# Attention projections on one core: queries stored per head, the first steps and the query pass in another order, weights' low parts on GpSimd

## The chip, the cores and the metric

The kernel runs as one program on one core of a Trainium2 chip. The metric is device time in microseconds (us), smaller is better. "Before" is the kernel as it stood, "after" the changed one. All times in this part come from the kernel before.

## The reference

Sequence 2048 plus 16 learned meta tokens in front (T = 2064), width 1024. Layer one is latent attention with a gate, layer two a gated short convolution; each ends in a layer norm with a residual.

```python
proj = h @ w_in                                    # 1024 -> 384 + 256 + 32 + 1024
c_q, c_kv, k_rope, z = split(proj)
q = (rms_norm(c_q, g_q) @ w_uq)                    # 16 heads x (64 + 32)
q = [q_nope, rope(q_rope)]
c_kv = rms_norm(c_kv, g_kv)
k_nope, v = c_kv @ w_uk, c_kv @ w_uv               # 16 heads x 64 each
k = [k_nope, rope(k_rope)]                         # one rope key for all heads
p = softmax(q k^T / sqrt(96), block-causal over chunks of 64)
out = (p v * silu(z)) @ w_o
h = layer_norm(alpha * h + out)
# then: in-projection to 4 x 1024, gates, a causal width-3 convolution, out-projection, layer norm
```

## The kernel before

Float32 products are made as three products of parts: a high part (`hi`, the value rounded to the engine's narrower format) and a low part (`lo = value - hi`); `split_matmul` (L41) issues hi x hi, hi x lo and lo x hi, all on TensorE. So every operand, inputs and weights, must be split before it is used: ScalarE (ACT) writes the high part as a copy, VectorE (DVE) subtracts for the low part.

Five stages follow one another: `stage_p` (projections), `stage_b` (attention), `stage_c` (output projection), `stage_d` and `stage_e` (the convolution layer). The change is in `stage_p` and in how `stage_b` loads queries.

**stage_p.** The 2064 tokens are eight chunks of 258 columns (`CA`, `NCA`). `STEPS_P` orders the work as p0, p1, o0, p2, o1, p3, o2, ...: step "p g" projects chunk g into the latents (three banks of 24 matmuls of 258 columns: `project`), step "o g" makes the outputs of pass g from its latents (`make`). g 0 to 7 is the key pass (two latent tiles and the rope key; eight key tiles and four or more value tiles out), g 8 to 15 the query pass (three latent tiles; eight query tiles "q" and four rope tiles "r" out), then eight "z" steps make the gates. Outputs go through a ring of four PSUM banks: output r waits until output r-4 has been taken out of its bank, by ACT or by DVE (`TAKER`), into one of eight stage slots, which the SP queue stores to DRAM. In the query pass the order is q q r q q r ...; ACT takes the q, DVE the r (four multiplications with the cos and sin tables `rot`).

Between p and o lies a chain over several engines: ACT copies the banks (`copies`), DVE squares (`squares`), TensorE sums over partitions (`mean_squares`), DVE adds epsilon (`mean_taken`), ACT takes the root (`root`), DVE inverts (`inverse`), does a Newton step of four operations (`newton`) and scales (`normalise`), ACT makes the high part and DVE the low part (`latent`). Each engine runs its instructions in the order in which they are written, so this order, with the waits in it, is written out by hand. For the rope key, DVE multiplies by cos and sin (`rotate_key`), ACT moves the sin half, DVE subtracts, and SP stores it (L299).

The cos and sin tables are made on the chip: a chain of DVE operations from the positions (L628 to L639), then four Sin activations on ACT (L405). In the kernel before they come ahead of the first step, and `copies(0)`, which frees the first banks, comes behind them on ACT.

The weights come in 30 pieces (`PIECES`), loaded by SP into four quarter buffers; the load of a piece waits until the piece before it in that buffer has its low part (`PIECE_FREE`, semaphore `w_split`). GpSimd (POOL) does nothing in this stage but two memsets.

**stage_b.** Per head, SP loads keys, then queries (four transfers: 64 plain rows, 32 cos rows, 16 and 16 sin rows) and values; GpSimd splits them for the next head while the current one runs. TensorE, ACT and DVE run in a written-out order. Each unit's output is added by DVE (L1165) into one of two halves of a buffer that SP stores (L910); the next but one waits for that store.

Of the kernel before, what the change touches and what calls it, by code (L numbers as in the profile page):

```python
# [6 lines left out]
F32 = mybir.dt.float32  # L7
F32R = mybir.dt.float32r
I32 = mybir.dt.int32
ALU = mybir.AluOpType  # L10
# [3 lines left out]
P = 128  # L14
# [140 lines left out]
FIRST_KEYS = 96  # L155
KEYS_IN, KEYS_SPLIT, QUERIES_IN, QUERIES_SPLIT = 2 * NCA + 1, 2 * NCA + 3, 2 * NCA + 4, 2 * NCA + 6


def load_queries(sp, raw, h, queries, semaphore):

    qn_d, qc_d, qs_d = queries
    at = 32 * (h % 4)
    sp.dma_start(raw[0:64, :], qn_d[h // 2, 64 * (h % 2):64 * (h % 2) + 64, :]).then_inc(semaphore, 16)
    sp.dma_start(raw[64:96, :], qc_d[h // 4, at:at + 32, :]).then_inc(semaphore, 16)
    sp.dma_start(raw[96:112, :], qs_d[h // 4, at + 16:at + 32, :]).then_inc(semaphore, 16)
    sp.dma_start(raw[112:P, :], qs_d[h // 4, at:at + 16, :]).then_inc(semaphore, 16)
# [9 lines left out]
def stage_p(nc, own, dram):  # L176

    x_a, w_x, w_uk, w_uv, w_uq, pos, rope_c, gains, ident_d, k_d, kr_d, v_d, queries, z_d = dram
# [3 lines left out]
    with ExitStack() as ctx:  # L182
# [70 lines left out]
        def _(sp):  # L253
# [14 lines left out]
            def store(r):  # L268
                kind, g, what, m, half, _ = OUTS[r]
                sp.wait_ge(taken[TAKER[r]], TAKEN[r])  # L270
                if what == "v":
                    t0, rows = value_tiles(g)[m]
                    to = v_d[t0:t0 + rows, half * HALF:half * HALF + HALF]
                else:
                    to = {"k": k_d, "q": queries[0], "r": queries[1], "z": z_d}[what][m, :, chunk_cols(g)]
                sp.dma_start(to, stage_of(r, rows_of(r))).then_inc(stored[SLOT[r]], 16)
                if what == "r":
                    sp.dma_start(queries[2][m, :, chunk_cols(g)], sines_of(r)).then_inc(stored[SLOT[r] + 1], 16)
# [11 lines left out]
            for i in range(3, 7):  # L290
                load_piece(i)
            next_piece = 7
            for kind, g in STEPS_P:
                if kind == "p":
                    if g == 1:
                        load_x(2)
                    if g < NCA:
                        sp.wait_ge(k_sum, g + 1)
                        sp.dma_start(kr_d[:, chunk_cols(g)], krs[0:32, :]).then_inc(kr_out, 16)  # L299
# [12 lines left out]
                if kind == "z" and g == KEYS_IN:  # L312
# [6 lines left out]
                    sp.dma_start(rot[96:P, :], kr_d).then_inc(first_in, 16)  # L319
# [3 lines left out]
                if kind == "z" and g == QUERIES_IN:  # L323
                    sp.wait_ge(first_split, 2)
                    load_queries(sp, rot, 0, queries, first_in)
# [8 lines left out]
        def _(pool):  # L334
            nc.gpsimd.memset(means[:, 0, :], 1.0 / KVL).then_inc(consts_set, 1)
            nc.gpsimd.memset(means[:, 1, :], 1.0 / QL).then_inc(consts_set, 1)

        @block.scalar
        def _(act):
# [17 lines left out]
            def copies(g):  # L357
                for j in range(tiles_of(g)):
# [3 lines left out]
                    nc.scalar.activation(craw[:, j, :], banks[:, j, 0:CA], ACT.Copy).then_inc(c_taken, 1)  # L362
                if g < NCA:
                    act.wait_ge(k_turned, g + 1)
# [28 lines left out]
            def first_queries():  # L393
                act.wait_ge(first_in, FIRST_KEYS + 64)
# [7 lines left out]
            act.wait_ge(angle, 1)  # L402
            for half in range(2):
                for part in range(2):
                    nc.scalar.activation(rot[64 * part:64 * part + 32, half * HALF_T:half * HALF_T + HALF_T],  # L405
                                         ang[64 * half + 32 * part:64 * half + 32 * part + 32, :], ACT.Sin).then_inc(sined, 1)
            for kind, g in STEPS_P:
                if kind == "p":
                    if g:
                        split_x(g + 1)  # L410
                    if g == 1:
                        root(0)
                        latent(0)
                    if g != 1:
                        split_weights(PIECES_AT.get((kind, g), ()))
                    copies(g)
                    if g == 1:
                        split_weights(PIECES_AT[kind, g])
# [30 lines left out]
        def _(pe):  # L449
            def bank_free(g, j):  # L450
# [3 lines left out]
                if g <= NCA and j == KKV:  # L454
                    pe.wait_ge(k_turned, g)
# [79 lines left out]
        def _(dve):  # L535
# [11 lines left out]
            def split_weights(pieces):  # L547
                for name, n in pieces:
                    i = PIECE[name, n]
                    dve.wait_ge(w_hi_done, i + 1)  # L550
                    nc.vector.tensor_tensor(piece_to(i, 1), piece_raw(i), piece_to(i, 0).bitcast(F32), ALU.subtract).then_inc(w_split, 1)
# [7 lines left out]

            def rotate_key(g):  # L560
                dve.wait_ge(proj, 3 * g + 3)
                if g == 0:
                    dve.wait_ge(sined, 4)
                for part in (0, 64):
                    last = nc.vector.tensor_tensor(kt[part:part + 32, :], banks[part:part + 32, 2, 0:CA], rot[part:part + 32, chunk_cols(g)], ALU.mult)
# [58 lines left out]
            split_weights([("x", 0)])  # L624
            split_half_x0(1)
            split_weights([("x", 1)])
# [4 lines left out]
            split_weights([("x", 2)])  # L631
            for part in (TURN1, TURN2, TURN3):
                then(nc.vector.scalar_tensor_tensor(ang, turns, -part, ang, ALU.mult, ALU.add))
            split_x(1)
            then(nc.vector.tensor_scalar(ang, ang, rc[:, 2:3], None, ALU.add))
# [4 lines left out]
            for kind, g in STEPS_P:  # L640
                extra = list(PIECES_AT.get((kind, g), ()))
                if kind == "p":
                    if g:
                        split_x(g + 1)
                    if g == 1:
# [3 lines left out]
                        normalise(0)  # L649
                        latent(0)  # L650
                    if g != 1:
                        split_weights(extra)
                    squares(g)
# [1127 lines left out]
```

## Time and profile before

| what | us |
|---|---|
| median of 3 runs | 2818.47 (2814.31 to 2821.31) |
| the profiled execution's own time | 2829.5 |
| span of its instructions | 2827.7 |
| TensorE's matmuls busy in the span | 2660.8 (94%) |
| VectorE, ScalarE, GpSimd busy | 1597.0 (56%), 1219.4 (43%), 752.2 (27%) |
| stage_p in it | 0 to about 618 |
| stage_b in it | about 618 to 1670 |

The profile is of one execution. PE is TensorE's matmuls, PEld its weight loads, SPq the transfer queue of SyncE. A row of the timeline gives start, duration, engine, line, operation, what it writes and reads, and in brackets how long the engine had been idle and what released it. "x2" merges neighbours.

### The profile page before, as it was taken

The numbers are of one execution on the slowest core, as the hardware profiler recorded it, in microseconds if no ns is written. First come the engines' busy times: TensorE is split into PE (matmuls) and PEld (weight loads), VectorE is DVE, ScalarE is ACT, GpSimd is POOL, SyncE is SP. The second block draws the span as 40 slices with busy tenths as digits, with TensorE's granted clock in tenths as the row PEclk, the third lists the DMA queues.
The fourth block names the chain that finished last, engine by engine and source line by source line (L and its number), as shares of the span: only waits on it lengthen the run. The fifth ranks groups of instructions, "written<-read, shape, count | busy, mean of one in ns | idle before, by whom it ended". The sixth has DMA issues, their size and how long they took to land. (4 is left out here: it accounts for less than half of the span.)

```text
span 2827.7 us, 45472 instructions
## 1 busy us (share of the span) xinstructions
PE 2660.8 (94%) x16756; PEld 2434.5 (86%) x16756; DVE 1597.0 (56%) x3262; ACT 1219.4 (43%) x3055; POOL 752.2 (27%) x332
## 2 busy tenths in 40 slices
PE   5998899999999999999999979969999999999898
PEld 5898899999888989898989858859988899889686
DVE  5556571129888878898988848854112111121465
ACT  4333222238887878887878841112111001110211
POOL 0000000013344544433444204441211111211244
PEclk8999999999999999999999989989999999999999
DMA  4545344312243334333333335643111011110543
GB/s 139 187 152 170 123 140 137 106 45 47 49 92 82 87 77 90 80 73 69 78 70 70 62 106 166 190 157 105 37 45 37 22 37 37 37 31 17 175 154 113
DMA packets 235457, 260.88 MB, mean 92 GB/s; under 512 B 86992, under 2 KB 188240, under 8 KB 228880
## 3 DMA queue, kind: packets, MB, share of 16 engines
q1 hardware_dynamic: 217600, 250.11, 32.3%
q10 hardware_dynamic: 17680, 8.46, 1.1%
q8 instruction: 106, 1.74, 0.3%
q14 instruction: 71, 0.58, 0.1%
HBM read 165.77 MB, written 92.20 MB: 91 GB/s over the span
## 5 line engine op out<-in xcount | busy, mean ns | idle before, releaser
L1159 DVE TENSOR_TENSOR b_pt_lo<-b_transposed,b_pt_hi 128x384 fp32r<-128x384 f32 (+4 forms) x784 | 429.2, 564 | 50.9 <-ACT b_pt_hi L1062 46.1
L1052 ACT ACTIVATE arena<-b_ring,b_nmax 128x384 f32<-128x384 f32 (+7 forms) x784 | 435.6, 560 | 49.9 <-DVE b_nmax L1151 41.1
L43 PE MATMUL d_ring<-d_h_hi,d_w_hi 128*128 128x410 f32 (+1 forms) x1152 | 426.0, 370 | 17.4 <-POOL d_w_lo L1465 15.7
L1062 ACT ACTIVATE b_pt_hi<-b_transposed 128x384 fp32r<-128x384 f32 (+4 forms) x784 | 382.1, 501 | 128.0 <-PE b_transposed L1092 115.8
L44 PE MATMUL d_ring<-d_h_lo,d_w_hi 128*128 128x410 f32 (+1 forms) x1152 | 426.7, 370 | 0.0
L45 PE MATMUL d_ring<-d_h_hi,d_w_lo 128*128 128x410 f32 (+1 forms) x1152 | 425.5, 369 | 0.0
L1146 DVE TENSOR_REDUCE b_cmax<-b_ring 128x1 f32<-128x384 f32 (+4 forms) x736 | 396.1, 542 | 36.0 <-PE b_ring L45 22.0
L1092 PE MATMUL b_transposed<-identity,arena 128*128 128x128 f32 (+2 forms) x2448 | 383.0, 274 | 18.0 <-DVE b_pt_lo L1159 14.6
L1109 PE MATMUL b_o_ps<-b_pt_hi,b_v 128*128 128x256 f32 (+2 forms) x1280 | 335.7, 293 | 19.0 <-DVE arena L1165 18.3
L1092 PEld LDWEIGHTS b_transposed<-identity,arena 128*128 128x128 f32 (+2 forms) x2448 | 280.8, 135 | 69.6 <-issue 40.1
L1110 PE MATMUL b_o_ps<-b_pt_lo,b_v 128*128 128x256 f32 (+2 forms) x1280 | 314.3, 282 | 0.0
L43 PE MATMUL b_ring<-region 128*128 128x384 f32 (+7 forms) x784 | 304.0, 388 | 3.1 <-DVE b_transposed L1122 2.4
L43 PE MATMUL p_banks<-p_x_hi,big_hi 128*128 128x258 f32 x896 | 256.6, 286 | 21.3 <-ACT arena L362 13.0
L1109 PEld LDWEIGHTS b_o_ps<-b_pt_hi,b_v 128*128 128x128 f32 x1280 | 243.1, 190 | 23.7 <-DVE arena L1165 21.1
L45 PE MATMUL b_ring<-region 128*128 128x384 f32 (+7 forms) x784 | 261.0, 333 | 0.0
L44 PE MATMUL b_ring<-region 128*128 128x384 f32 (+7 forms) x784 | 260.4, 332 | 0.0
L45 PE MATMUL p_banks<-p_x_hi,big_lo 128*128 128x258 f32 x896 | 256.3, 286 | 0.0
L44 PE MATMUL p_banks<-p_x_lo,big_hi 128*128 128x258 f32 x896 | 255.8, 285 | 0.0
L43 PEld LDWEIGHTS d_ring<-d_h_hi,d_w_hi 128*128 128x128 f32 x1152 | 217.4, 189 | 41.6 <-issue 18.3
L1110 PEld LDWEIGHTS b_o_ps<-b_pt_lo,b_v 128*128 128x128 f32 x1280 | 244.3, 191 | 0.7
L45 PEld LDWEIGHTS d_ring<-d_h_hi,d_w_lo 128*128 128x128 f32 x1152 | 217.6, 189 | 22.2
L44 PEld LDWEIGHTS d_ring<-d_h_lo,d_w_hi 128*128 128x128 f32 x1152 | 217.2, 189 | 22.5
(165 smaller groups left out, 4882.9 us busy)
## 6 DMA issues: line engine op xcount, KB each, us to landing
arena<-x_a SPq DMA_DIRECT2D x23, 1032.0 KB, 5.5
d_w_st<-w_conv SPq DMA_DIRECT2D x32, 512.0 KB, 3.4
keys<-arena SPq DMA_DIRECT2D x64, 129.0 KB, 5.2
queries<-arena SPq DMA_DIRECT2D x64, 129.0 KB, 3.0
gates<-arena SPq DMA_DIRECT2D x64, 129.0 KB, 2.2
arena<-keys SPq DMA_DIRECT2D x16, 516.0 KB, 4.8
arena<-queries SPq DMA_DIRECT2D x16, 516.0 KB, 8.9
values<-arena SPq DMA_DIRECT2D x32, 256.0 KB, 2.2
```

The lines of the kernel that those rows point to most:

```text
L43: nc.tensor.matmul(out, w_hi, x_hi, start=start, stop=False)
L44: nc.tensor.matmul(out, w_hi, x_lo, start=False, stop=False)
L45: return nc.tensor.matmul(out, w_lo, x_hi, start=False, stop=stop)
L1052: nc.scalar.activation(p[0:rows, n % PSLOTS, 0:w], banks[0:rows, n % RING, 0:w], ACT.Exp, bias=nmax[0:rows, tile % 8:tile % 8 + 1], accum_ ...
L1062: nc.scalar.activation(turned(pt_hi, g, u, nb)[:, :, tile_columns(u, j)], tb[:, n % 2, 0:nb, 0:rows], ACT.Copy).then_inc(pt_hi_done, 1)
L1092: last = nc.tensor.transpose(tb[0:keys, n % 2, c, 0:rows], p[0:rows, s % PSLOTS, col:col + keys], ident[0:rows, 0:rows])
L1109: nc.tensor.matmul(ob[:, part], v[:, h % 2, vb, :], turned(pt_hi, n, u, len(blocks))[:, c, part], start=(x == 0 and c == 0), stop=False)
L1110: last = nc.tensor.matmul(ob[:, part], v[:, h % 2, vb, :], turned(pt_lo, n, u, len(blocks))[:, c, part], start=False, stop=end)
L1146: ins = nc.vector.tensor_reduce(top, bank[0:rows, 0:w], AX, ALU.max, negate=(chunks == 1))
L1159: nc.vector.tensor_tensor(lo, tb[:, n % 2, 0:nb, 0:rows], hi.bitcast(F32), ALU.subtract).then_inc(pt_split, 1)
```

## The change

1. Queries are stored in one DRAM tensor `q_d[head, 128, T]`, with 64 plain, 32 cos and 32 sin rows for each head, in place of three tensors. The stores of a q tile and of an r tile write two and four heads' rows; their number is as before. A head's queries are loaded in one transfer in place of four. For the sums to match, the rope key's second copy is loaded with its halves swapped (one more transfer, once).
2. The low parts of all weight pieces but the first are made by GpSimd, in piece order, in place of DVE.
3. The first steps: `copies(0)` and the splits of uk come ahead of the Sin activations on ACT, which now come in step p1 behind `copies(1)` and the splits of uv; the key shifts of chunks 0 and 1 come behind them. On DVE, `squares(0)` and a copy of the first rope key out of its bank (`keep_key`) come ahead of the last five operations of the angle chain; both keys are rotated in step p1. `load_x(2)` is issued ahead of the uv pieces.
4. The query pass on DVE: the second r tile is taken ahead of the Newton step in place of behind it.

```diff
-def load_queries(sp, raw, h, queries, semaphore):
-    qn_d, qc_d, qs_d = queries
-    at = 32 * (h % 4)
-    sp.dma_start(raw[0:64, :], qn_d[h // 2, 64 * (h % 2):64 * (h % 2) + 64, :])...
-    sp.dma_start(raw[64:96, :], qc_d[h // 4, at:at + 32, :])...
-    sp.dma_start(raw[96:112, :], qs_d[h // 4, at + 16:at + 32, :])...
-    sp.dma_start(raw[112:P, :], qs_d[h // 4, at:at + 16, :])...
...
+                elif what == "q":
+                    to = q_d[2 * m:2 * m + 2, 0:64, chunk_cols(g)]
+                elif what == "r":
+                    to = q_d[4 * m:4 * m + 4, 64:96, chunk_cols(g)]
...
-            for i in range(3, 7):
-                load_piece(i)
+            load_piece(3)
+            load_piece(4)
+            load_x(2)
+            load_piece(5)
+            load_piece(6)
...
-                    if g == 1:
-                        load_x(2)
-                    if g < NCA:
-                        sp.wait_ge(k_sum, g + 1)
-                        sp.dma_start(kr_d[:, chunk_cols(g)], krs[0:32, :]).then_inc(kr_out, 16)
+                    for c in {0: (), 1: (0, 1)}.get(g, (g,) if g < NCA else ()):
+                        sp.wait_ge(k_sum, c + 1)
+                        sp.dma_start(kr_d[:, chunk_cols(c)], krs[0:32, :]).then_inc(kr_out, 16)
...
+            for i in range(len(PIECES)):                     # GpSimd
+                pool.wait_ge(w_hi_done, i + 1)
+                pool.wait_ge(w_split, i)
+                if i:
+                    nc.gpsimd.tensor_tensor(piece_to(i, 1), piece_raw(i), piece_to(i, 0).bitcast(F32), ALU.subtract).then_inc(w_split, 1)
...
             split_x(1)                                       # ACT
-            act.wait_ge(angle, 1)
-            for half in range(2):
-                ... four Sin activations
+            copies(0)
+            split_weights(PIECES_AT["p", 0])
...
                     if g == 1:
                         root(0)
+                        split_x(2)
                         latent(0)
+                        copies(1)
+                        split_weights(PIECES_AT["p", 1])
+                        act.wait_ge(angle, 1)
+                        ... four Sin activations
+                        shift_key(0)
+                        shift_key(1)
+                        continue
...
+            def keep_key():                                  # DVE
+                dve.wait_ge(proj, 3)
+                nc.vector.tensor_copy(kt, banks[:, 2, 0:CA]).then_inc(k_turned, 1)
...
-            for part in (TURN1, TURN2, TURN3):
+            for part in (TURN1, TURN2):
                 then(nc.vector.scalar_tensor_tensor(ang, turns, -part, ang, ALU.mult, ALU.add))
             split_x(1)
+            squares(0)
+            keep_key()
+            then(nc.vector.scalar_tensor_tensor(ang, turns, -TURN3, ang, ALU.mult, ALU.add))
...
                     if g == 1:
                         mean_taken(0)
                         inverse(0)
                         newton(0)
                         normalise(0)
+                        split_x(2)
                         latent(0)
                     squares(g)
+                    if g == 1:
+                        rotate_key(0)
                     if g < NCA:
                         rotate_key(g)
...
                     take(mine[0])                            # query pass
-                    split_weights(extra[0:2])
                     if chain:
                         inverse(g + 1)
+                    take(mine[1])
+                    if chain:
                         newton(g + 1)
-                    take(mine[1])
-                    split_weights(extra[2:])
-                    if chain:
                         normalise(g + 1)
                     take(mine[2])
...
-                load_queries(sp, raw, h + 1, queries, raw_in)     # stage_b
+                sp.dma_start(raw[:, :], q_d[h + 1]).then_inc(raw_in, 16)
```

## Rows read from the trace of the kernel before

**Rows 1.** Busy time in one stretch; then clock granted (1.00 is 2.4 GHz), DMA share, GB/s.
```profile
40.00:60.00 20.00, 9.33 (x59) 8.75 (x58) 12.37 (x18) 7.62 (x10) 0.00 (x0) 0.74 0.12 30
```
**Rows 2.** Timeline of PE, the first steps: matmuls that ended an idle time.
```profile
32.04 0.55 PE L43 MATMUL p_banks<-p_x_hi,big_hi 128*128 128x258 f32 x1 [13.02 <-ACT arena L362]
...
53.37 0.58 PE L43 MATMUL p_banks<-region 128*128 128x258 f32 x1 [9.61 <-DVE region L594]
...
60.10 0.36 PE L43 MATMUL p_banks<-region 128*128 128x258 f32 x1 [1.15 <-DVE arena L606]
```
**Rows 3.** Timeline of ACT, the first steps.
```profile
15.18 1.93 ACT L343 ACTIVATE p_x_hi<-arena 128x2064 fp32r<-128x2064 f32 x1 [1.42 <-DMA arena<-x_a]
...
17.13 1.28 ACT L405 ACT_TABLE_LOAD   x1
...
25.28 4.31 ACT L405 ACTIVATE arena<-arena 32x1032 f32<-32x1032 f32 x4 [6.87 <-DVE arena L639]
...
42.31 1.93 ACT L343 ACTIVATE p_x_hi<-arena 128x2064 fp32r<-128x2064 f32 x1 [7.42 <-DMA arena<-x_a]
```
**Rows 4.** Timeline of DVE, the first steps.
```profile
18.81 2.31 DVE L545 TENSOR_TENSOR p_x_lo<-arena,p_x_hi 128x2064 fp32r<-128x2064 f32 x1
21.03 0.75 DVE L635 TENSOR_SCALAR arena<-arena,p_rc 128x1032 f32<-128x1032 f32 x1
...
46.61 0.43 DVE L574 TENSOR_SCALAR arena<-p_banks 128x258 f32<-128x258 f32 x1
...
59.52 0.43 DVE L606 COPY arena<-p_banks 128x258 f32<-128x258 f32 x1
```
**Rows 5.** Timeline of PE, key and query pass: matmuls that ended an idle time.
```profile
110.64 0.50 PE L43 MATMUL p_banks<-region 128*128 128x512 f32 x1 [1.63 <-DVE arena L606]
...
248.53 0.58 PE L43 MATMUL p_banks<-region 128*128 128x258 f32 x1 [3.80 <-DVE region L551]
...
277.55 0.40 PE L43 MATMUL p_banks<-region 128*128 128x258 f32 x1 [3.56 <-DVE arena L603]
...
384.45 0.40 PE L43 MATMUL p_banks<-region 128*128 128x258 f32 x1 [0.68 <-DVE arena L603]
...
408.36 0.39 PE L43 MATMUL p_banks<-region 128*128 128x258 f32 x1 [0.63 <-DVE arena L603]
...
426.84 0.58 PE L43 MATMUL p_banks<-region 128*128 128x258 f32 x1 [1.83 <-ACT arena L380]
```
**Rows 6.** Timeline of DVE in step o9 of the query pass.
```profile
271.11 1.23 DVE L551 TENSOR_TENSOR big_lo<-arena,big_hi 128x1024 fp32r<-128x1024 f32 x1 [1.77 <-ACT big_hi L355]
272.25 1.76 DVE L578 RECIPROCAL arena<-arena 128x258 f32<-128x258 f32 x1
...
275.76 1.74 DVE L603 TENSOR_TENSOR arena<-p_banks,arena 64x258 f32<-64x258 f32 x4
```
**Rows 7.** Group of POOL instructions by form: busy us, mean ns, idle before.
```profile
L1019 POOL TENSOR_TENSOR big_lo<-arena,big_hi 128x1024 fp32r<-128x1024 f32 x8 | 19.3, 2414 | 0.6
```
**Rows 8.** Timelines of POOL and DVE in stage_c; last, a DVE group by form.
```profile
1743.26 3.31 POOL L1268 TENSOR_TENSOR c_y<-c_y,c_ln 128x1024 f32<-128x1024 f32 x1 [6.00 <-DVE c_y L1186]
...
1744.23 2.49 DVE L1352 TENSOR_TENSOR c_z<-c_z,c_r 128x128 f32<-128x128 f32 x1
...
L1359 DVE TENSOR_TENSOR c_gt_lo<-c_g,c_gt_hi 128x128 fp32r<-128x128 f32 x1 | 0.3, 293 | 0.4 <-ACT c_gt_hi L1279 0.4
```
**Rows 9.** Waits of PE in stage_b; transfers: number, KB each, us to landing.
```profile
PE b_o_ps L1109 <- DVE arena L1165: 18.3, 11, 3.5
...
arena<-x_a SPq DMA_DIRECT2D x23, 1032.0 KB, 5.5
...
arena<-keys SPq DMA_DIRECT2D x16, 516.0 KB, 4.8
arena<-queries SPq DMA_DIRECT2D x16, 516.0 KB, 8.9
...
arena<-sin_queries SPq DMA_DIRECT2D x32, 129.0 KB, 10.2
```

More of the change, by code:

```diff
@@ L176, in stage_p @@
 def stage_p(nc, own, dram):
-    x_a, w_x, w_uk, w_uv, w_uq, pos, rope_c, gains, ident_d, k_d, kr_d, v_d, queries, z_d = dram
+    x_a, w_x, w_uk, w_uv, w_uq, pos, rope_c, gains, ident_d, k_d, kr_d, v_d, q_d, z_d = dram
     wx_hi, wx_lo, region, rot, stage = own.big_hi, own.big_lo, own.region, own.rot, own.stage
@@ L318, in _ @@
                     sp.dma_start(rot[64:96, :], kr_d).then_inc(first_in, 16)
-                    sp.dma_start(rot[96:P, :], kr_d).then_inc(first_in, 16)
+                    for half in range(2):
+                        sp.dma_start(rot[96 + 16 * half:112 + 16 * half, :], kr_d[16 - 16 * half:32 - 16 * half, :]).then_inc(first_in, 16)
                     sp.dma_start(rot[0:64, :], k_d[0, 0:64, :]).then_inc(first_in, 16)
@@ L401, in _ @@
             split_x(1)
[L402 to L406 removed]
+            copies(0)
+            split_weights(PIECES_AT["p", 0])
             for kind, g in STEPS_P:
                 if kind == "p":
[L409 to L410 removed]
+                    if g == 0:
+                        continue
                     if g == 1:
                         root(0)
+                        split_x(2)
                         latent(0)
[L414 to L415 removed]
+                        copies(1)
+                        split_weights(PIECES_AT["p", 1])
+                        act.wait_ge(angle, 1)
+                        for half in range(2):
+                            for part in range(2):
+                                nc.scalar.activation(rot[64 * part:64 * part + 32, half * HALF_T:half * HALF_T + HALF_T],
+                                                     ang[64 * half + 32 * part:64 * half + 32 * part + 32, :], ACT.Sin).then_inc(sined, 1)
+                        shift_key(0)
+                        shift_key(1)
+                        continue
+                    split_x(g + 1)
+                    split_weights(PIECES_AT.get((kind, g), ()))
                     copies(g)
[L417 to L418 removed]
+                    shift_key(g)
                 else:
@@ L640, in _ @@
             for kind, g in STEPS_P:
[L641 removed]
                 if kind == "p":
[L643 to L644 removed]
+                    if g == 0:
+                        continue
                     if g == 1:
@@ L699, in _ @@
                     take(r)
-                split_weights(extra[0:2])
                 if chain:
@@ L704, in _ @@
                     take(r)
-                split_weights(extra[2:3])
                 if chain:
@@ L711, in _ @@
                     latent(g + 1)
-                for n, r in enumerate(mine[first + 4:]):
+                for r in mine[first + 4:]:
                     take(r)
-                    split_weights(extra[3 + n:4 + n])
 PSLOTS = 14
@@ L1761, in program @@
             own = own_memory(nc, inner, ident, big_hi, big_lo)
-            stage_p(nc, own, [ins[n] for n in ("x_a", "w_x", "w_uk", "w_uv", "w_uq", "pos", "rope_c", "gains", "ident")] + [k_d, kr_d, v_d, queries, z_d])
-            stage_b(nc, own, [k_d, v_d, queries, z_d, ins["w_o"], o_d, r_d, og_d])
+            stage_p(nc, own, [ins[n] for n in ("x_a", "w_x", "w_uk", "w_uv", "w_uq", "pos", "rope_c", "gains", "ident")] + [k_d, kr_d, v_d, q_d, z_d])
+            stage_b(nc, own, [k_d, v_d, q_d, z_d, ins["w_o"], o_d, r_d, og_d])
         stage_c(nc, ident, big_hi, big_lo, [ins["x_rows"], og_d, o_d, z_d, r_d, ins["ln"][0], h_d, h_t_d])
```

51 lines of the change are left out of this document (23 added, 28 removed).

## Prediction

> **What bounds the kernel now.** The page comes first (the table above): TensorE's matmuls fill 94% of the span, so the kernel can only gain where TensorE idles or runs at its lower clock. Cutting the span into stretches shows where that is. In stage_p, TensorE is busy 9.33 of the 20 us from 40 to 60, at a mean granted clock of 0.74, so in part at 1.2 GHz [rows 1]. The timeline of PE in the first 70 us then shows two long holes, 13.02 us and 9.61 us, and a small one of 1.15 us at 60.10, behind which no hole is over 0.9 us until 110 [rows 2]. The timelines of ACT and DVE tell what filled them. The 13.02 us wait is for the first bank copies on ACT, which stand behind the four Sin activations [rows 3]. The 9.61 us wait is for the first latent; its chain starts with the mean at 46.61 on DVE, behind the split of the third x, whose data came only at 42.31 [rows 3, 4]. Later, in the query pass, one hole of 3.80 us and three of 3.5 us like the one at 277.55 stand in front of matmuls released by DVE [rows 5]. The waits in stage_b show 18.3 us in 11 waits for DVE's output addition, which itself waits for an output store [rows 9].
>
> **First steps.** Worked out from when the data is there. ACT has x(1)'s high part at 15.18 + 1.93 = 17.1 as before, and copies the banks right then. DVE, whose earlier low parts moved to GpSimd, can split x(1) from 17.1 on (before 18.81), to 19.4. TensorE ends p0 near 19.0 (32.04 - 13.02) and goes on with p1 at 19.4 instead of 32.04. That alone isn't the gain: TensorE next needs the first latent. On DVE behind 19.4: squares 0.7 (an estimate from the 1.23 us of a 1024-column operation [rows 6], with 516 columns), key copy 0.43, one angle operation 1.25 (same row), the four others and the clamp, which took from 21.03 until 25.25 when Sin could start, 4.2 [rows 3, 4]: 26.0. x(2) is issued at 19.4 and needs 5.5 us [rows 9], so it is there at 25, in time. The chain from the mean to the latent took 46.61 to 53.3 = 6.7 [rows 2, 4]; now 2.31 for x(2)'s low part lie in it, of which 0.7 cover a wait for ACT: 26.0 + 8.3 = 34.4. So o0 can start at 34.4 instead of 53.37.
>
> But it stalls again after four outputs, since their first bank is emptied by DVE (L606), which is now behind both key rotations, and these need Sin. On ACT, copies(1), 0.7, follows the latent (35.3), then two uv high parts, 2.0 together (from 1.93 for the same number of columns), until 37.3; table load 1.28, Sin 4.31: 42.9 [rows 3]. The first rotation is two multiplications, ACT's shift and a subtraction, some 0.43 us each for 258 columns (as the row at 46.61 [rows 4]), 1.75 with the hand-overs; the second as much plus about 1 for the store of the first sum, which uses the same buffer: 42.9 + 1.75 + 2.75 = 47.4. So the first key tile is taken at 47.4 instead of 59.52: 12.1 us earlier. From there the order of the steps is the old one. Before, the hole in front of 60.10 was 1.15 us and TensorE came out of it at full clock (0.36 us a matmul, against 0.55 and 0.58 behind long holes [rows 2]); now it waits some 7 us there and starts at 1.2 GHz. What this costs, about 2 us, I take from the query pass below. Leaves 10.
>
> **Low parts on GpSimd.** One of 1024 columns takes 2.41 us there [rows 7] against 1.23 us on DVE [rows 6]. Do they also hold DVE up? In stage_c a DVE operation of 128 columns took 2.49 us beside a GpSimd operation, and the GpSimd one 3.31 us, where the same size of DVE operation takes 0.29 alone [rows 8]. So a DVE operation with two inputs from SBUF does wait for a GpSimd one, up to all of its 2.41 us. The Trainium skill states this as a rule (SBUF — State Buffer, section "SBUF: two separate sides"): the pair of ports that the two share is an exclusive lock, held for the whole instruction. By it the move would take nothing off DVE where both are busy, and the time would be that of rival A below; these rows agree with it.
>
> In the first steps, two or three GpSimd operations (w2, uk0, uk1) meet DVE's angle chain, which sets the path. No delay would leave 10; two full ones, 4.8, leave 5. I take 2: **gain 8, bounds 3 to 11** (11 if the clock costs only 1).
>
> In the key pass, x3/x4, x5/x6 and x7 are split in o2 to o4, where TensorE waited 1.63 (at 110.64 [rows 5]), again 1.65 and 0.5 us for DVE's take behind the Newton step. DVE loses 2.4 us of own work in o2 but may wait 4.8 in the Newton step, so that the hole grows by 2.2; in o3 the take slips in between, gain 1.2; o4 gain 0.3. SP waits for these low parts too, and the key stores are queued behind it, 1.2 to 2.4 us later; ACT needs their slots, which may delay the next square sum by 1. **Loss 1, bounds loss 5 to gain 4.**
>
> **Query pass.** In step o9, DVE does the weight's low part (271.11), the reciprocal (272.25) and Newton, then takes the second r tile at 275.76 until 277.5, the moment TensorE goes on [rows 5, 6]. That tile was made near 270.8: TensorE makes an output (9 matmuls) in 1.08 us and wanted its bank at 274.0. Three outputs earlier, near 267.5, the first r tile was made; its take ends at 269.3, the reciprocal then at 271.1, and with the second take right behind it and no low part between, this one ends at 272.9, ahead of 274.0. So the 3.56 hole and its like go; GpSimd's operation then meets the Newton step, which has a whole projection, 8.6 us, of slack. From 248.53 to 408.36 lie six periods, 159.8 us. A period with nothing but its own small hole is 408.36 - 384.45 = 23.9, without the hole 23.3 [rows 5]. Six of these are 139.7: 20.1 us saved. The holes in it sum to about 12.6 (three of 3.5 to 3.6, three of 0.6 to 0.7); the other 7.5 us follow the four long ones, 1.9 each, and are matmuls at the lower clock, 0.58 us against 0.39 for the first ones [rows 5]: the price used above. In o8 the 3.80 us at 248.53 shrink to about 1.1, since uq8 to uq11 are no longer queued behind DVE's chain: gain 2.7. Against it: the uq loads come up to 1 us later, for GpSimd is slower (about 1.0 for 384 columns, an estimate from 2.41 for 1024): loss 1. The last latent comes 0.7 later. In o15, x13's load waits for x11's low part on GpSimd, 1.2 later, and ACT's takes are behind that piece; TensorE already waited 1.83 us there at 426.84 [rows 5]: loss 1.2. **Gain 20, bounds 13 to 23.**
>
> **Per-head queries.** The stores are as many, of the same bytes and rows: 0. In stage_b one transfer of 1032 KB, 128 rows, replaces four. The x loads of that shape land in 5.5 us; the first of the four, 516 KB, in 8.9 and the last in 10.2, but a keys load of 516 KB alone in 4.8 [rows 9], so much of this is sharing with the values' load and with what is still queued. The output store is issued behind all of them, and TensorE's 11 waits (18.3 us, the longest 3.5) end with it. If it lands 1 us earlier, up to 9 us are saved; with 2 us, 15; if the queue is bound by bytes, nothing; if 1 us later, 15 heads lose 15. The queue moves the same bytes, so I stay near nothing: **gain 4, bounds loss 5 to gain 15.** SP has three issues fewer per head. The extra keys transfer in z is covered by TensorE's gate matmuls, which no wait interrupts there.
>
> **Sum.** 8 - 1 + 20 + 4 = 31 us, from the profiled execution's 2829.5 to 2798.5. That execution lay 11 us above the median of the runs; the saving doesn't depend on that, so 2818.5 - 31 = 2787.5, call it **2788**. What can be told from no change is about 0.3%, 8.5 us.
>
> **The rivals.**
> A: GpSimd holds DVE up wherever the two meet, as in stage_c: all DVE operations with two SBUF inputs wait up to 2.4 us. First steps gain 3, keys lose 5, query pass gains 13, stage_b 0: 11 us, 2807. For it: [rows 8]. Against: after o4 each step holds but one GpSimd operation, with slack behind it. Chance 0.15. (The Trainium skill's rule, named above, is this case.)
> B: the output store in stage_b is what counts. With one transfer the queue is free some 2 us earlier and most of the 18.3 us go: 27 + 15 = 42, 2776. For it: 5.5 against 10.2 us; against it: same bytes. Chance 0.2.
> C: slower. The single 1032 KB transfer goes ahead of values and output store as one block, and the store lands later in all 15 heads. The rest gains 27, so it decides from 27 / 15 = 1.8 us per head on; at 2.8 us the time is 2818.5 - 27 + 42 = 2833. Against it: same bytes, fewer issues. Chance 0.04.
> D: the change doesn't do what it says: the holes move on to the next taker, and only the first steps gain, 8 us, 2810. Against it: DVE had time at the end of each query step. Chance 0.06.
> The forecast: 0.55, its own range 2780 to 2797.
>
> **Range and chances.** 2770 to 2809 holds A, B and the bounds of the terms that are likely together. Faster by over 0.3%: the forecast, A, B and half of D, 0.92 with rounding; within: 0.05; slower: 0.03.
>
> **What would show it.** Right: p1 starts near 19.5, o0 near 35 to 39, the first key tile is taken (the L606 of before) near 47 to 52; no Sin ahead of 36. Query steps in periods of 23 to 24 us with no hole over 1 us; GpSimd operations of 2.4 us or more with 29 low parts in all; stage_b as long as before within 5 us. Wrong: holes in o2 of over 3 us, DVE operations of 258 columns that take 2 us and more (A); an output store that lands at another time, or L1165 waiting much more or less for it (B, C); holes of 3 us still there in o9 to o11 (D).

## The result, and the profile after

The changed kernel takes 2914.8 us (median of 4 runs, 2911.3 to 2917.7), the kernel before 2819.8 beside it (2814.3 to 2821.3). The ratio is 1.034, 95% interval 1.0321 to 1.0359: 95 us slower, where 31 us less were forecast. The profiled execution has a span of 2915.9 us. Its page begins with busy time, share of the span and instructions of each engine:

```profile
span 2915.9 us, 45463 instructions
## 1 busy us (share of the span) xinstructions
PE 2700.4 (93%) x16756; PEld 2466.1 (85%) x16756; DVE 1592.5 (55%) x3234; ACT 1218.3 (42%) x3056; POOL 807.9 (28%) x361
```

No engine got busier in a way that explains 88 us more of span: TensorE has 40 us more, and the rest is idle time. The first attention copy on ACT, which ends stage_p, starts at 729.80 us after and at 619.41 before. So stage_p lost 110 us, and the rest of the program gained 15 by the medians (22 between the two profiled executions, but that of before lay 11 us above its median and that of after 3). One step of the query pass, from one mean-square sum to the next (389.15 to 429.59), as a stretch of busy times:

```profile
core 0: us, PE busy (x) PEld busy (x) DVE busy (x) ACT busy (x) POOL busy (x), PEclk, DMA share, GB/s
389.15:429.59 40.44, 29.52 (x186) 27.64 (x186) 16.00 (x28) 6.99 (x14) 0.00 (x0) 0.79 0.25 79
```

That is 40.4 us for a step that took 23.8 before. TensorE isn't full, its granted clock is 0.79 of 2.4 GHz, DVE and ACT are far from full, and the DMA engines look nearly idle, at 0.25. The list of waits names what is missing (engine, line, who was waited for; us, times, the longest):

```profile
ACT arena L383 <- DMA queries<-arena: 208.2, 57, 8.4
...
DVE arena L620 <- DMA queries<-arena: 168.3, 27, 9.7
```

Both takers wait for a stage slot, and the slot for the query store that empties it. The stores' own row gives the duration of the issue on SP's queue as min/median/max in ns:

```profile
L270 SPq DMA_DIRECT2D queries<-arena x96: 489/2966/4417, 233.9 to 553.6; - x96
L270 SPq DMA_DIRECT2D keys<-arena x64: 319/440/1714, 53.3 to 218.2; - x64
```

Same line, same 129 KB: a key store holds the queue for 0.44 us, a query store for 2.97. The queue's timeline in that step shows nothing else:

```profile
396.97 8.59 SPq L270 DMA_DIRECT2D queries<-arena  x3
405.60 1.54 SPq L272 DMA_DIRECT2D queries<-arena  x1
407.18 7.57 SPq L270 DMA_DIRECT2D queries<-arena  x3
414.80 2.02 SPq L272 DMA_DIRECT2D queries<-arena  x1
416.87 7.68 SPq L270 DMA_DIRECT2D queries<-arena  x3
424.59 1.54 SPq L272 DMA_DIRECT2D queries<-arena  x1
426.17 7.57 SPq L270 DMA_DIRECT2D queries<-arena  x3
```

From 396.97 to 433.74 the issues stand end to end. SP's queue, with what serves it, is the bound of the query pass, a resource that no term of the sum had.

The other parts answer to [rows 2] and [rows 5]. TensorE's holes after, in the first steps and in o2:

```profile
21.83 0.39 PE L43 MATMUL p_banks<-p_x_hi,big_hi 128*128 128x258 f32 x1 [2.28 <-DVE p_x_lo L555]
40.27 0.58 PE L43 MATMUL p_banks<-region 128*128 128x258 f32 x1 [7.09 <-DVE region L611]
53.05 0.55 PE L43 MATMUL p_banks<-region 128*128 128x258 f32 x1 [5.93 <-DVE arena L623]
...
106.68 0.50 PE L43 MATMUL p_banks<-region 128*128 128x512 f32 x1 [3.24 <-DVE arena L623]
```

The 13.02 us hole became 2.28, and 9.61 became 7.09; the third is new at 5.93 (about 7 had been forecast) and the one in o2 grew from 1.63 to 3.24. Line numbers moved: in after the key and value takes are L623, the r takes L620, the output addition of stage_b L1178.

The starts of the mean-square sums place the gains and losses; "e1" and "e4" are experiments below. One column is the start in o1, o4, o8 and o14 of stage_p, the last the end of the stage, in us:

| kernel | o1 | o4 | o8 | o14 | end |
|---|---|---|---|---|---|
| before | 78.8 | 147.1 | 236.1 | 398.7 | 619.4 |
| after | 73.3 | 144.9 | 235.4 | 470.0 | 729.8 |
| e1 | 73.5 | 145.0 | 235.5 | 375.7 | 596.4 |
| e4 | 72.8 | 144.1 | 234.6 | 374.9 | 596.9 |
| e6 | 73.9 | 144.2 | 234.7 | 390.6 | 612.7 |
| e7 | 69.6 | 137.7 | 226.6 | 377.3 | 596.6 |
| e8 | 71.2 | 139.5 | 230.0 | 370.3 | 591.9 |

Up to the sum in o8 the change is ahead, as e1 and e4 are. Everything is lost behind it, in the steps that store queries. Each row is one execution; the kernels with the same first steps (after, e1, e4, e6) reach o1 between 72.8 and 73.9, so a difference of about 1 us in one column says nothing.

### The profile page after: what moved, and what is told of

The parts are those of the page before. It is cut to its first block and busy times, and to the rows that moved or that the text cites. A ratio compares the mean times of both kernels' runs of the same rounds, so it can differ in the third digit from the quotient of the medians.

```text
span 2915.9 us, 45463 instructions
## 1 busy us (share of the span) xinstructions
PE 2700.4 (93%) x16756; PEld 2466.1 (85%) x16756; DVE 1592.5 (55%) x3234; ACT 1218.3 (42%) x3056; POOL 807.9 (28%) x361
## 5 line engine op out<-in xcount | busy, mean ns | idle before, releaser
L43 PE MATMUL p_banks<-p_x_hi,big_hi 128*128 128x258 f32 x896 | 260.8, 291 | 13.3 <-DVE big_lo L559 8.3
L43 PE MATMUL p_banks<-region 128*128 128x258 f32 (+2 forms) x484 | 169.7, 351 | 89.6 <-ACT arena L383 35.9
L383 ACT ACTIVATE arena<-p_banks 128x258 f32<-128x258 f32 (+2 forms) x194 | 80.7, 422 | 382.9 <-DMA queries<-arena 208.2
```

The costliest lines, as they stand in the source:

```text
L43: nc.tensor.matmul(out, w_hi, x_hi, start=start, stop=False)
L383: nc.scalar.activation(stage_of(r, rows), bank_of(r, rows), ACT.Silu if OUTS[r][2] == "z" else ACT.Copy, scale=SCALE if OUTS[r][2] == "q" ...
```

## The experiments

The theory (P): a store is slow when its outermost extent is small. `q_d[2m:2m+2, 0:64, cols]` has the same rows and bytes as a flat tile, but 2 outermost parts, and `q_d[4m:4m+4, 64:96, cols]` has 4. (The expectations of e1 to e5 call this theory S, and those of e9 and e10 call it P.) The rivals: the new order or the low parts on GpSimd cost the time (rival L of e1 and e2); or what is slow is writing into the one large tensor, in whatever shape (rival P of e3 and e4). The kernel before took 2802.6 us beside e1 to e4 and 2804.6 beside e6 to e10; ratios go by these, and kernels of different sets are compared by their ratios: after at 1.034 would stand at 2898 where e4 stands at 2768. The times expected of e1 to e4 were set before these runs, beside a before of 2819.8. On that scale the ratios put e1 at 2798, e3 at 2783 and e4 at 2785, inside theory S's ranges, and e2 at 2922, 7 us above its range.

### e1: part 1 undone

```diff
-                elif what == "q":
-                    to = q_d[2 * m:2 * m + 2, 0:64, chunk_cols(g)]
+                    to = {"k": k_d, "q": queries[0], "r": queries[1], "z": z_d}[what][m, :, chunk_cols(g)]
...
-                sp.dma_start(raw[:, :], q_d[h + 1]).then_inc(raw_in, 16)
+                load_queries(sp, raw, h + 1, queries, raw_in)
```

> The changed kernel with the queries' DRAM layout, stores and loads of the kernel before; the new first steps, the new query order and GpSimd's low parts stay. Theory S (the stores' shape, two or four outermost parts, is what costs, some 125 us in the query pass, while the single load saves some 20 us in stage_b): query pass in periods near 23.3 us, stage_b as before, 2795 to 2802. Rival L (GpSimd's low parts or the new order cost it): stays above 2880.

2780.5 us, ratio 0.9922 [0.9906, 0.9939], 22 us faster than before. Parts 2 to 4 are worth 22 us; the forecast for them was 27. No hole is left in o9 to o14 and the steps take 22.9 us.

### e2: part 1 alone, on the kernel before

```diff
-                load_queries(sp, raw, h + 1, queries, raw_in)
+                sp.dma_start(raw[:, :], q_d[h + 1]).then_inc(raw_in, 16)
...
+                    to = q_d[2 * m:2 * m + 2, 0:64, chunk_cols(g)]
...
+                    to = q_d[4 * m:4 * m + 4, 64:96, chunk_cols(g)]
```

> The kernel before with nothing but the new layout: one tensor per head, its stores and its single load. Theory S: query pass longer by some 100 us (each step bound by the queue, near 40 us), stage_b some 20 us shorter: 2890 to 2915. Rival L: within 10 us of before.

2904.0 us, 1.0361 [1.0343, 1.0378], with stage_p's end at 729.99. The layout carries the whole loss, and the order and GpSimd none of it: the first rival is out.

### e3: the same bytes as flat rows

```diff
-                    to = q_d[2 * m:2 * m + 2, 0:64, chunk_cols(g)]
+                    to = q_d[2 * m, :, chunk_cols(g)]
...
-                    to = q_d[4 * m:4 * m + 4, 64:96, chunk_cols(g)]
+                    to = q_d[4 * m + 1, :, chunk_cols(g)]
```

The sines' store is likewise flat, into head 4m + 3. Rows land at other places than the reference wants, so the times alone count.

> The changed kernel, but each stored query tile goes as 128 rows into one head's place (q tile m to head 2m, cos to 4m + 1, sin to 4m + 3): same number of transfers, bytes and row length, the plain two-dimensional shape, wrong places, so the queries it computes with are not the reference's. Theory S: the stores cost no more than before and the single load keeps its gain, 2770 to 2785. Rival P (the cost is the head-wise tensor in DRAM itself, however it is written): no faster than 2880.

2765.2 us, 0.987 [0.9854, 0.9887]. The same tensor, bytes, number of stores and loads, and 0.047 of 2803, so 132 us, faster than the change. It is the shape, and not the tensor. The issue of a query store is back at a median of 0.43 us.

### e4: the walk turned round

The columns of the weights' q part are permuted on their way in, so that a tile's rows alternate between two heads; the store then walks 64 rows outermost and 2 heads inside. The r and sine stores keep their 4 parts.

```diff
-                    to = q_d[2 * m:2 * m + 2, 0:64, chunk_cols(g)]
+                    to = q_d[2 * m:2 * m + 2, 0:64, chunk_cols(g)].rearrange("h p t -> p h t")
...
-    nope, rope = uq[..., :NOPE].reshape(KQ, P, PAIRS, P), ...
+    nope, rope = uq[..., :NOPE].reshape(KQ, P, PAIRS, 2, NOPE).transpose(0, 1, 2, 4, 3).reshape(KQ, P, PAIRS, P), ...
```

> The changed kernel with the 128 columns of each plain query tile taken in another order from the weights (the two heads' columns alternate), so that the same rows go to the same places in DRAM, but the transfer's outermost part has 64 members and not 2; the cos and sin stores keep their 4. Theory S: the 64 plain stores are cheap again, the 64 rope stores keep about 1.5 us of queue each, 12 us a step, which fits under a step's 23 us: 2770 to 2790. Rival P (places or head-wise tensor count): above 2880.

2767.8 us, 0.9875 [0.9859, 0.9892]: 35 us faster than before, and nothing of the reference is left out. The order of the store's walk is worth 1.034 - 0.9875 of 2803 us, so 130 us; the ends of stage_p, 729.8 and 596.9, say 133. TensorE is full in the step, at full clock, with the same work and the 4-part stores beside it; the view is again the stretch of busy times:

```profile
329.00:352.00 23.00, 23.00 (x189) 22.83 (x188) 16.09 (x28) 7.11 (x14) 0.00 (x0) 1.00 0.46 141
```

### e5: the shapes alone

A program that does nothing but store one 129 KB tile in several shapes, first one at a time, then eight in a row, with 16 plain output stores behind; it computes nothing of the reference.

```python
def place(t, a, n):                       # a outermost parts; 0: 64 rows outermost
    if a == 0: return t[0:2, 0:64, cols].rearrange("h p t -> p h t")
    if a == 1: return t[0, :, cols]
    return t[0:a, 0:P // a, cols]
```

> No part of the reference is computed: the kernel only stores the same 128 x 258 tile (129 KB) to DRAM in six shapes, alone (three each) and in bursts of eight, and writes some rows of x as output. Shapes: 128 rows flat; 2 parts of 64 rows; 4 of 32; 8 of 16; 16 of 8; and 64 rows outermost with two members. Theory S (few engines carry a store whose outermost part is small): alone, the 2-part store lands several us later than the flat one, 4 parts less late, 16 parts and 64-outermost as the flat one; in bursts the time for each falls in proportion to the parts, some 3 to 4 us for 2 parts, half for 4, down to the flat one's 0.5 at 16. Rival W (the row length or the places matter): all six alike.

Stretches of the bursts of eight: 2, 4, 8 and 16 outermost parts, then 64 rows outermost, then flat (stretch, length, an idle engine, clock, DMA share, GB/s):

```profile
63.80:91.30 27.50, 0.00 (x0) 1.00 0.13 38
91.30:106.30 15.00, 0.00 (x0) 1.00 0.23 70
106.30:114.80 8.50, 0.00 (x0) 1.00 0.40 124
114.80:125.30 10.50, 0.00 (x0) 1.00 0.42 101
125.30:132.40 7.10, 0.00 (x0) 1.00 0.45 149
58.00:63.80 5.80, 0.00 (x0) 1.00 0.55 182
```

By these stretches a store in 2 parts takes 27.5 / 8 = 3.4 us, in 4 parts 1.9, in 8 parts 1.1, 64 rows outermost 0.9, flat 0.7. This is one execution. The column to look at is the DMA share, the mean over 16 engines: 0.13 with 2 parts is two engines of sixteen at work all the time, and 0.23 with 4 parts is four. Bytes per time follow: 38, 70 and 124 GB/s with 2, 4 and 8 parts, 182 flat. The Trainium skill (DMA: Bandwidth & Descriptors, section "Why a DMA increments its semaphore by 16 and not by 1") states it: a transfer is carried by the largest number of engines up to 16 that divides the outermost non-unit extent of both access patterns. The trace agrees: the share says so at 2 and at 4, and beside its 128 rows each store shows as many packets of under 512 B as the rule names engines (16, 32, 64, 128, 128 and 128 of them in the six bursts of eight, in the order above). Alone, from start to start with the landing in between, a 2-part store takes 5.1 us (9.72, 14.91, 19.99 on SP's timeline), then 3.5, 2.8, 2.4 and 2.3 for 4, 8 and 16 parts and 64 rows, and a flat one 1.9 (three from 4.16, the next at 9.72).

Each stretch above also holds the wait ahead of its first packet and the last landing. From first to last packet the bursts of 2 and 4 parts, of 8 and 16, of 64 rows and flat are shorter:

```profile
65.00:90.80 25.80, 0.00 (x0) 1.00 0.13 41
92.40:105.70 13.30, 0.00 (x0) 1.00 0.26 79
107.40:114.30 6.90, 0.00 (x0) 1.00 0.50 153
116.00:122.10 6.10, 0.00 (x0) 1.00 0.72 173
126.50:131.60 5.10, 0.00 (x0) 1.00 0.62 207
58.80:62.90 4.10, 0.00 (x0) 1.00 0.78 258
```

So a store behind others costs 3.2 us in 2 parts, 1.7 in 4, 0.9 in 8, 0.8 in 16, 0.6 with 64 rows outermost and 0.5 flat. Theory S's forecast of 3 to 4 us, half of that at 4 and 0.5 flat came true; 16 parts and 64 rows were a little dearer than flat, not equal to it.

### e9: two parts alone

The change with its r and sine stores walked 32 rows outermost (rows of four heads in another order than the reference wants), and the q stores left in 2 parts.

```diff
-                    to = q_d[4 * m:4 * m + 4, 64:96, chunk_cols(g)]
+                    to = q_d[4 * m:4 * m + 4, 64:96, chunk_cols(g)].rearrange("h p t -> p h t")
```

> This is the changed kernel with one alteration: its 64 stores of parts r and their 32 of sines put the same bytes on the same places of the queries' tensor, but walk them row by row, so that the outermost extent is 32 and not 4 (the 32 rows of the four heads land in another order than the reference wants; the time is what counts). The 64 stores of two heads' first rows are left as they were, in 2 outermost parts. Theory P (what makes a store slow is the number of its outermost parts; those of 2 are carried by two of the DMA engines at 3.4 us each and set the query pass): the step of the query pass stays at 36 to 40 us, stage_p ends at 700 to 730 us, and the kernel takes 2885 to 2915 us, 1.027 to 1.04 of the kernel before. Theory T (the stores of 4 parts carry the cost, or both do in equal parts): the step falls to 23 to 32 us and the kernel takes 2765 to 2850 us.

2834.5 us, 1.0105 [1.0088, 1.0122]. (The expectation counts 64 r stores; there are 32, and 32 of sines.) P, which had the 2-part stores carry everything, missed by 50 us. T's ranges were met, the time and the step of 31.0 us, and the 2-part stores alone do cost half of the loss against e4 (66 of 133 us by the ends of stage_p, 662.7 here). But T's picture of two costs that add up fails too, for the 4-part stores alone cost nothing that shows (e4 beside e3). What explains both is a queue that serves one store behind the other, with a price of its own for each shape, hidden up to TensorE's 22.9 us a step. A query step has 8 q, 4 r and 4 sine stores:

| kernel | stores at e5's stretches, us | sum | sum by e5's packets alone | step measured |
|---|---|---|---|---|
| change | 8 x 3.4 + 8 x 1.9 | 42.4 | 25.8 + 13.3 = 39.1 | 40.4 |
| e9 | 8 x 3.4 + 8 x 0.9 | 34.4 | 25.8 + 5.1 = 30.9 | 31.0 |
| e4 | 8 x 0.9 + 8 x 1.9 | 22.4 | 5.1 + 13.3 = 18.4 | 22.9, TensorE's |
| e3 | 16 x 0.7 | 11.2 | 4.1 + 4.1 = 8.2 | 22.9, TensorE's |

e9's step is read off SP's timeline, where the loads of x mark its ends:

```profile
359.65 0.58 SPq L253 DMA_DIRECT2D arena<-x_a  x1
360.27 8.42 SPq L270 DMA_DIRECT2D queries<-arena  x3
368.73 0.60 SPq L272 DMA_DIRECT2D queries<-arena  x1
...
390.69 0.58 SPq L253 DMA_DIRECT2D arena<-x_a  x1
```

The sine store went from 1.5 to 0.6 us of issue by its shape alone. The first sums come out 2 and 3 us high, since each price holds a share of a burst's first wait and last landing; by the packets alone they are within 1.3 us. Neither holds the step's load of x. e4 stays under TensorE's step by both. Whether these prices are those of SP's queue or of the two and four DMA engines behind it isn't shown: the same stores from another engine's queue were not tried.

### e10: the layout with the good walk, on the kernel before

```diff
+                    to = q_d[2 * m:2 * m + 2, 0:64, chunk_cols(g)].rearrange("h p t -> p h t")
...
+                sp.dma_start(raw[:, :], q_d[h + 1]).then_inc(raw_in, 16)
```

> The kernel before with one part of the change alone, the queries in one tensor and one load for a head, and with the two heads' first rows interleaved in the weights' columns, so that these stores walk 64 rows outermost. No reordering, all low parts of the weights on VectorE. Theory P (the layout cost its time by the stores' 2 outermost parts alone, and the single load is worth its 12 to 16 us in stage_b): stage_p ends within 2 us of the kernel before's 619 us and the kernel takes 2786 to 2794 us, 0.9935 to 0.996 of the kernel before. Rival M (one row of 128 partitions over two heads still costs something, or the single load gains only together with the earlier end of stage_p): 2796 to 2812 us, no difference from the kernel before or slightly slower.

2791.0 us, 0.9952 [0.9935, 0.9968]: 13.6 us faster, as forecast for theory P. Its stage_p ends at 622.9 against 619.4 in the run shown of before, 3.5 later (more than the 2 allowed), so what follows stage_p gives about 17, an estimate over two sets of runs. The 3.5 us arise behind o14, which both reach within 0.1 us, for the most part in one wait of TensorE for DVE that the trace of before doesn't have; DVE in turn had waited for a store of queries, which points at the 4-part stores as not quite free there:

```profile
432.26 0.55 PE L43 MATMUL p_banks<-p_x_hi,big_hi 128*128 128x258 f32 x1 [3.00 <-DVE arena L598]
430.38 1.74 DVE L598 TENSOR_TENSOR arena<-p_banks,arena 64x258 f32<-64x258 f32 x4 [2.62 <-DMA queries<-arena]
```

In stage_b it is the wait of [rows 9] that went: TensorE's waits for DVE's output addition, of after, e1 and e3 in this order:

```profile
L1122 PE MATMUL b_o_ps<-b_pt_hi,b_v 128*128 128x256 f32 (+2 forms) x1280 | 335.5, 293 | 5.1 <-DVE arena L1178 4.4 <-DVE b_pt_lo L1172 0.7
```
```profile
PE b_o_ps L1127 <- DVE arena L1183: 10.1, 6, 3.6
```
```profile
L1122 PE MATMUL b_o_ps<-b_pt_hi,b_v 128*128 128x256 f32 (+2 forms) x1280 | 333.7, 291 | 1.7 <-DVE arena L1178 1.0 <-DVE b_pt_lo L1172 0.7
```

Before it was 18.3. With one transfer for a head 4.4, 1.0 (e3) and 0.6 (e10) are left.

The timelines of SP's queue show why. Here is one head's loads and the output store behind them, in e1 (four transfers of queries) and in e3 (one):

```profile
683.26 0.47 SPq L163 DMA_DIRECT2D arena<-queries  x1
...
686.53 11.40 SPq L928 DMA_DIRECT2D o_t<-arena  x3
```
```profile
683.65 0.32 SPq L903 DMA_DIRECT2D arena<-queries  x1
...
684.96 13.24 SPq L923 DMA_DIRECT2D o_t<-arena  x3
```

In the median over 15 heads the output store is issued 5.2 us behind the first query issue in e1 (6.1 before) and 1.3 us behind it in e3, and lands 14.2 us (15.6 before) against 11.4 us behind it. DVE's waits for that store fall from 17.4 us in e1 to 2.0 in e3.

### e6, e7, e8: order and low parts, on e4

e6 takes the second r tile behind the Newton step again; e7 makes all low parts of weights on DVE; e8 makes those before the uq pieces on DVE and the rest on GpSimd.

```diff
                     if chain:                             # e6
                         inverse(g + 1)
-                    take(mine[1])
-                    if chain:
                         newton(g + 1)
+                    take(mine[1])
+                    if chain:
                         normalise(g + 1)
...
-                if i:                                     # e7, e8 (GpSimd)
+                if i >= FIRST_POOL:                       # 30 in e7, the first uq piece in e8
...
+                    if i < FIRST_POOL:                    # e7, e8 (DVE)
+                        dve.wait_ge(w_hi_done, i + 1)
+                        nc.vector.tensor_tensor(piece_to(i, 1), piece_raw(i), ...).then_inc(w_split, 1)
```

> e4 with the query pass on DVE in its old order (Newton step ahead of the second rope tile's take), low parts still on GpSimd. Theory O (order alone removes the holes of o9 to o11): the 3.5 us holes shrink only by the low part's share, about 1.2 us each, and 0.6 stays in each step: 8 to 14 us slower than e4, 2776 to 2784 on the scale of 2802.6 for before. Rival G (moving the low parts did it): within 3 us of e4.

> e4 with all low parts back on DVE, in the new orders. Theory K (GpSimd's operations hold DVE up for their whole length): in the first steps DVE's angle chain is 3 to 4 us shorter, the first key tile is taken earlier by as much, the hole in o2 goes from 3.2 back to 1.6 us; the query pass loses at most 5 us in o8 and o9 to o11. 2762 to 2772. Rival: GpSimd takes work off DVE and that is the gain: 2780 and more.

> e7 with the low parts of the pieces from uq on (query pass) on GpSimd and those before on DVE. Theory K: the better of both in each pass, 2758 to 2766, some 3 to 6 us under e4. Rival: no different from e4.

e6: 2784.2 us, 0.9936 [0.9917, 0.9955], 16 us above e4 (0.0061 of 2804 by the ratios: 17), just over the 8 to 14 of theory O; rival G is out. The place of the one take is most of what the query pass gained. Holes of 2.7 to 2.9 us stand in o9 to o11 and of 0.6 to 0.7 behind:

```profile
272.11 0.39 PE L43 MATMUL p_banks<-region 128*128 128x258 f32 x1 [2.74 <-DVE arena L620]
```

GpSimd's low part alone cuts the hole only from 3.56 [rows 5] to 2.74, since its instruction now meets the Newton step. On DVE's timeline of e6 two multiplications of the same size take 0.43 and 2.49 us, the second one beside a GpSimd low part from 267.59 to 270.00:

```profile
267.00 0.43 DVE L599 TENSOR_TENSOR arena<-arena 128x258 f32<-128x258 f32 x1
267.46 0.30 DVE L600 TENSOR_SCALAR arena<-arena 128x258 f32<-128x258 f32 x1
267.79 2.49 DVE L601 TENSOR_TENSOR arena<-arena 128x258 f32<-128x258 f32 x1
```

e7: 2772.0 us, 0.989 [0.9871, 0.9908], not told apart from e4. GpSimd's low parts are worth nothing as a whole, because what they gain in the query pass they had lost before it: by the table above, e7 is 8.0 us ahead of e4 at o8 and 2.4 behind at o14. The hole in o2 is back at 1.64 us, as forecast, but the query pass lost 10.4 us where at most 5 were allowed. e8 keeps most of both (e7 is 3.4 us ahead of it at o8): 2764.8 us, 0.9854 [0.9838, 0.9871], the fastest measured, 3 us under e4 and 40 us below the kernel before. Its interval overlaps e4's, so that it beats e4 rests on the trace alone (stage_p's end at 591.9 against 596.9).

## Why the prediction was wrong

**The step that failed** stands under Per-head queries: "The stores are as many, of the same bytes and rows: 0." All three counts are right, and the price isn't made of them. In the step's place, the runs showed that a 129 KB store costs SP's queue 3.2 to 3.4 us in 2 parts and 1.7 to 1.9 in 4, against 0.5 to 0.7 flat, and that the 16 stores of a query step are served one behind the other: 39 to 42 us by those prices where 23 were free. Against the same order with harmless stores (e4) the change loses 130 us; less e4's gain of 35 that is the 95 measured. Two things in the prediction's own material should have raised the question. It weighed the load's shape (128 rows in one against 64, 32 and 16) and didn't look at the store's; and it left out SP's queue when it named what bounds the query pass, although every slot that ACT and DVE fill is emptied there.

**First steps**, forecast gain 8, bounds 3 to 11. Measured 5.3 at o1 (73.5 against 78.8, e1). TensorE came out of its wait for the latent at 40.27 where 34.4 was forecast, and the first key tile was taken at 52.47 where 47.4 was. The second half of the chain, behind Sin, went as worked out; all of the 5 us were lost before it. DVE's timeline after, with GpSimd's low parts from 10.37, 13.65 and 20.78 (2.38, 2.69 and 6.03 for two):

```profile
11.39 1.92 DVE L644 TENSOR_SCALAR arena<-arena,p_rc 128x1032 f32<-128x1032 int32 x1 [1.79 <-DMA arena<-pos]
...
14.13 2.77 DVE L646 TENSOR_SCALAR arena<-arena 128x1032 f32<-128x1032 f32 x1
...
21.70 2.88 DVE L566 TENSOR_TENSOR arena<-arena 128x516 f32<-128x516 f32 x1
...
24.83 3.06 DVE L652 SCALAR_TENSOR_TENSOR arena<-arena 128x1032 f32<-128x1032 f32 x1
```

In e7, without GpSimd, these four take 0.76, 0.70, 0.69 and 1.23: 7.3 us lost where 2 were taken for it and 4.8 was the bound. Four operations were hit, not two, since the two uk pieces come back to back and catch DVE twice.

**Keys**, forecast loss 1, bounds loss 5 to gain 4. Between o1 and o4 the lead fell from 5.3 to 2.1 (e1), a loss of 3.2. The hole in o2 grew from 1.63 to 3.24, by 1.6 where "grows by 2.2" stood. By o8 another 1.5 was gone, 4.7 in all. In bounds, mis-sized.

**Query pass**, forecast gain 20, bounds 13 to 23. In e1 the lead goes from 0.6 at o8 to 23.0 at o14: 22.4. The mechanism (take ahead of Newton, holes and the slow matmuls behind them gone) is shown by e6 and e4. In the change itself this gain is buried under the stores.

**Stage_b**, forecast gain 4, bounds loss 5 to gain 15. e1 against e3 gives 15.4, e1 against e4 12.7, e10 against before 13.6. The likelier bound was rival B, which is right in its mechanism: the output store is no longer late, and TensorE's waits for it fall from 18.3 to 4.4 us after, 0.6 in e10. The landing times by themselves mislead here: the one big load takes a median of 9.6 us after and 8.3 in e3, the parts before 8.9 to 10.2, but each part counts from its own issue. From a head's first query issue until all its queries are in, the median is 12.4 us before and 11.4 in e1, against 7.9 in e3. The saving isn't in bytes, which are the same; it is in how soon the queue gets to the output store (1.3 us in place of 5.2). The prediction had weighed a landing 1 or 2 us earlier; it was 2.8 (14.2 to 11.4). Why the queue holds the values' load and the store less behind one issue than behind four isn't shown.

With the stores mended, 2788 was forecast at a before of 2818.5, a saving of 31; e4 saves 34.7. That these are so near is in part luck: first steps and keys together came out about 6 us lower than forecast, stage_b 9 to 11 higher.

**The rivals.** A (GpSimd holds DVE up) is real for the first steps and keys, not for the query pass. C and D didn't happen. The case that did, "slower by the stores", had no chance of its own; the 0.03 for slower was far too small for a change that rewrites the destination of 128 transfers.

## What to carry to other kernels

When a change regroups a tensor in DRAM, write down the outermost extent of every store and load that touches it, on both sides, and not only bytes and count; if it is 2 or 4, permute so that rows go outermost (the permutation is free when it can be put into a weight's columns). Add up the queue's time per step at the price of each shape and hold it against the busiest engine's, since stores that are harmless alone (the 4-part ones in e4) cost half of the loss beside the 2-part ones. Work moved to GpSimd should be put where DVE has slack; in a chain that sets the path, keep it on DVE.

## What the runs showed of the hardware that was not expected

Over a burst of eight with its last landing, 129 KB stores move at 38 GB/s in 2 outermost parts, 70 in 4, 124 in 8 and 182 flat (e5). 16 parts look worse than 8 there (101 GB/s), but while packets flow they move 173 GB/s against 153. The rest is 3.2 us between the last packet, by 122.1, and the next issue at 125.34, which waits for the landing; behind the other shapes it is 0.5 to 1.0 us, and why is open. A low DMA share (0.25 in the slow step) was here the sign of a bound queue, not of a free one.

DVE was held up by GpSimd in an operation with one SBUF input too: 2.77 us for a scalar operation of 1032 columns that takes 0.70 alone, and in o2 of the change 2.32 us for one of 258 that takes 0.30. The prediction had it for two inputs only. The Trainium skill (SBUF — State Buffer, section "SBUF: two separate sides") names a fast mode of DVE beside the two inputs; these rows agree with it in that an instruction of one input waits. The copy out of PSUM at 24.50 in the first steps kept its 0.41 us though it ran in the midst of a GpSimd low part (24.16 to 26.80).
